# Attention scores of a two-block transformer: the low half of the keys read on 64 partitions instead of on 128 padded with zeros

## The reference

```python
# block 1: 8 query heads, 2 key heads, head dim 64, a window of 128 keys
scores = jnp.einsum("bnqhgd,bnkhd->bnhgqk", q, kw).astype(jnp.float32) * ATTN_SCALE
...
# block 2: 2 layers, 8 heads of head dim 64, chunks of 64, 8 chunks to the left
scores = jnp.einsum("bnqhd,bnkhd->bnhqk", qc, kb) * (dh ** -0.5)
...
scores = jnp.where(valid, scores + bias[None, None], NEG_INF)
p = jax.nn.softmax(scores, axis=-1)
```

## Time and profile before

| | |
|---|---|
| median of 3 runs | 1238.54 us (1238.12 to 1240.27) |
| the profiled execution, its own time | 1238.12 us |
| its span, first to last instruction | 1236.3 us |
| time outside the span | 1.8 us |
| PE busy | 1207.9 us, 98% of the span |
| DVE, ACT, POOL busy | 844.2, 555.0, 351.5 us |
| attention of block 1, layer 0 and layer 1 of block 2 | 54 to 108 us, 721 to 830 us, 992 to 1102 us |

### The profile page before, as it was taken

One profiled execution on the slowest core, in us unless ns is written; L12 is line 12 of the kernel. 1 busy time (PEld: TensorE's weight loads), 2 busy tenths in 40 slices (PEclk: granted clock), 3 DMA queues, 4 the chain that ended last, 5 costly groups with the idle time before them and its releaser, 6 DMA issues.

```text
span 1236.3 us, 15052 instructions
## 1 busy us (share of the span) xinstructions
PE 1207.9 (98%) x5844; PEld 1013.3 (82%) x5844; DVE 844.2 (68%) x1532; ACT 555.0 (45%) x965; POOL 351.5 (28%) x267
## 2 busy tenths in 40 slices
PE   7999999999989999999999899999999999999997
PEld 6888888888877888888888689888888889888886
DVE  6778433436788836663668967777967766778964
ACT  6667332324434313342434455644334556553433
POOL 0155000002299991000002763343103033342000
PEclk9999999999999999999999999999999999999999
DMA  5322233223323332333223242322122332222221
GB/s 193 106 69 69 85 103 99 89 85 104 109 69 98 107 102 85 102 102 97 80 75 107 86 129 87 92 89 92 61 85 86 120 102 86 87 86 93 72 74 69
DMA packets 36152, 115.33 MB, mean 93 GB/s; under 512 B 3824, under 2 KB 6384, under 8 KB 36080
## 3 DMA queue, kind: packets, MB, share of 16 engines
q1 hardware_dynamic: 36080, 114.36, 29.3%
HBM read 112.25 MB, written 2.10 MB: 92 GB/s over the span
## 4 chain that ended last, share of the span: by engine, by line
PE 67%; DVE 20%; ACT 8%; issue 3%; POOL 1%; DMA 1%; SPq 0%; ACTq 0%
PE ps L273 65%; DVE RA L250 8%; DVE FA L262 6%; DVE FA L250 5%; ACT RA L242 4%; ACT FA L247 1%; ACT RA L246 1%; POOL FA L250 1%; DVE FA L1269 1%; PE ps L1303 1%; ACT FA L246 1%; DMA FA<-x 1%; DVE RA L262 1%; PE ps L747 0%; DVE FA L1273 0%
## 5 line engine op out<-in xcount | busy, mean ns | idle before, releaser
L273 PE MATMUL ps<-RA 128*128 128x512 f32 (+3 forms) x5460 | 1179.0, 376 | 11.6 <-DVE RA L250 9.3
L273 PEld LDWEIGHTS ps<-RA 128*128 128x128 f32 x5460 | 970.6, 188 | 197.3 <-DVE RA L250 11.1
L250 DVE TENSOR_TENSOR RA<-FA,RA 128x1024 fp32r<-128x1024 f32 (+4 forms) x316 | 334.8, 1068 | 185.7 <-ACT RA L242 183.5
L242 ACT ACTIVATE RA<-FA 128x1024 fp32r<-128x1024 f32 (+6 forms) x336 | 279.1, 860 | 340.4 <-PE ps L273 159.1
L250 POOL TENSOR_TENSOR FA<-FA 128x512 f32<-128x512 f32 (+1 forms) x89 | 123.2, 1384 | 549.5 <-ACT FA L246 450.6
L266 POOL TENSOR_SCALAR FA<-FA 128x256 f32<-128x256 f32 (+2 forms) x117 | 146.9, 1266 | 189.4 <-DVE FA L270 188.3
L262 DVE SCALAR_TENSOR_TENSOR FA<-ps,FA 128x512 f32<-128x512 f32 (+3 forms) x137 | 98.0, 721 | 87.6 <-PE ps L273 44.9
L247 ACT ACTIVATE FA<-FA 128x512 f32<-128x512 f32 (+3 forms) x113 | 61.2, 543 | 98.7 <-DVE FA L1273 78.3
L262 DVE SCALAR_TENSOR_TENSOR FA<-FA 128x4 f32<-128x4 f32 (+4 forms) x166 | 87.5, 535 | 17.8 <-ACT FA L246 6.5
L246 ACT ACTIVATE FA<-ps,FA 128x512 f32<-128x512 f32 x61 | 41.6, 686 | 120.3 <-PE ps L273 120.2
L246 ACT ACTIVATE FA<-FA 128x512 f32<-128x512 f32 (+3 forms) x74 | 41.5, 568 | 63.0 <-DVE FA L262 56.1
(11 more groups left out here) (46 smaller groups left out, 306.4 us busy)
## 6 DMA issues: line engine op xcount, KB each, us to landing
FA<-w_units SPq DMA_DIRECT2D x190, 512.0 KB, 3.5
FA<-rel SPq DMA_DIRECT2D x16, 256.0 KB, 3.4
FA<-w_units SPq DMA_DIRECT2D x8, 384.0 KB, 3.0
FA<-x SPq DMA_DIRECT2D x4, 512.0 KB, 7.7
FA<-dmat SPq DMA_DIRECT2D x8, 256.0 KB, 3.2
out<-FA SPq DMA_DIRECT2D x8, 256.0 KB, 2.2
FA<-gain SPq DMA_DIRECT2D x1, 512.0 KB, 3.5
FA<-positions SPq DMA_DIRECT2D x1, 256.0 KB, 3.9
```

Of the source, the lines that this page charges most:

```text
L242: return lambda eng: eng.activation(dst, src, ACT.Copy)
L250: return lambda eng: eng.tensor_tensor(dst, a, b, op)
L273: return lambda e: e.matmul(dst, a, b, start=start, stop=stop_)
```

## The change

`stacked_scores` gets the number of the head and reads both operands of its second pass on 64 partitions only: the half that holds the queries' high part and the keys' low part. The other half no longer needs zeros, so head A's and head B's low keys lie in one K2 of 512 columns, on its two halves; the memsets, their helper and the waits for them go. The tiles move together by 1024 columns, and the program takes the default size for a scratch area of transfers issued by software, of which it has none, in place of 1024 bytes.

```diff
-QA, QB, K1A, K1B, VV = Z + 8192, Z + 10240, Z + 12288, Z + 12800, Z + 13824
-K2A, K2B = Z + 13312, Z + 25856
+QA, QB, K1A, K1B, K2, VV = Z + 8192, Z + 10240, Z + 12288, Z + 12800, Z + 13312, Z + 13824
...
-K2P = Z + 20480
-P2H, P2L = Z + 22528, Z + 24192
-YAH, YAL = Z + 25856, Z + 27904
-R_COLS = Z + 29952
+P2H, P2L = Z + 21504, Z + 23168
+YAH, YAL = Z + 24832, Z + 26880
+R_COLS = Z + 28928
...
-        def zero(name, c, n, after):
-            G(name, after, lambda e: e.memset(Rf(c, n), 0.0))
...
-        zero("z1a", K2A, 512, [])
-        zero("z1", K2B, 512, [])
...
-                V(f"{key}.l{n}", [f"{key}.h3", zeroed], fn)
+                V(f"{key}.l{n}", [f"{key}.h3"], fn)
...
-        def stacked_scores(o, q, k1, k2, i, k0, nk, after, name):
+        def stacked_scores(o, q, k1, k2, head, i, k0, nk, after, name):
+            p = 64 * head
             T(None, after, mmul(o, R(q + 128 * i, 128), R(k1 + k0, nk), True, False))
-            T(name, [], mmul(o, R(q + 128 * i, 128), R(k2 + k0, nk), False, True))
+            T(name, [], mmul(o, R(q + 128 * i, 128, p, p + 64), R(k2 + k0, nk, p, p + 64), False, True))
...
-        zero("z2", K2P, 2048, ["gemm.br7"])
...
-                base, lows = QK + 2048 * (i % 2), K2P + 1024 * (i % 2)
-                return [base + 512 * n for n in range(4)] + [lows, lows + 512]
+                base = QK + 2560 * (i % 2)
+                return [base + 512 * n for n in range(5)]
...
-    nc = _bacc.Bacc("TRN2", target_bir_lowering=False, num_devices=1, dynamic_dma_scratch_size=1024)
+    nc = _bacc.Bacc("TRN2", target_bir_lowering=False, num_devices=1)
```

More of the change, by code:

```diff
@@ L610, in stacked_q, with stacked_k @@
             free(f"bank{b}" if src is None else src[1], f"{key}.l1")
-        def stacked_k(key, b, k1a, k1b, k2a, k2b, after, zeroed, bias=None):
+        def stacked_k(key, b, k1a, k1b, k2, after, bias=None):
             n = 0
@@ L622, in stacked_k @@
             yield
-            for n, (k1, k2, p) in enumerate(((k1a, k2a, 0), (k1b, k2b, 64))):
+            for n, (k1, p) in enumerate(((k1a, 0), (k1b, 64))):
                 src = bank(b, 512, 0, p, p + 64)
@@ L687, in q_evacuate @@
             yield from stacked_q(f"q{m}", qb[m], QA + 512 * m, QB + 512 * m, [f"qn.{m}"], bin_ + m, src=(t, tn))
-        k_split = stacked_k("k", 5, K1A, K1B, K2A, K2B, ["gemm.k"], "z1", bin_ + 4)
+        k_split = stacked_k("k", 5, K1A, K1B, K2, ["gemm.k"], bin_ + 4)
         staggered([q_evacuate(0), q_evacuate(1), k_split, q_evacuate(2), q_evacuate(3)])
@@ L709, in a_scores @@
                     after = after + ["k.l1", "q3.l1"]
-                stacked_scores(bank(b, nk, 256 * (t % 2)), (QA, QB)[g] + 512 * t, (K1A, K1B)[g], (K2A, K2B)[g], n,
+                stacked_scores(bank(b, nk, 256 * (t % 2)), (QA, QB)[g] + 512 * t, (K1A, K1B)[g], K2, g, n,
                                k0, nk, after, f"S.{s}.{t}")
@@ L1197, in evac_qk @@
                     else:
-                        yield from stacked_k(key, b, cols[2], cols[3], cols[4], cols[5], after + room, "z2")
+                        yield from stacked_k(key, b, cols[2], cols[3], cols[4], after + room)
                     return
@@ L1243, in half_scores @@
                         after = after + [f"{l}q{item}.l1", f"{l}k{item}.l1"]
-                        stacked_scores(bank(b, w), cols[h % 2], cols[2 + h % 2], cols[4 + h % 2], i, 0, w, after, name)
+                        stacked_scores(bank(b, w), cols[h % 2], cols[2 + h % 2], cols[4], h % 2, i, 0, w, after, name)
                     else:
```

## The result

The changed kernel takes 1272.14 us (median of 4 runs, 1272.07 to 1272.27) against 1238.49 us: 33.65 us more, a ratio of 1.0271 with a 95% interval of 1.0256 to 1.0286. The forecast was 1258.0 us in a range of 1238.0 to 1289.5. The sign held and the time lies in the range, but the increase is 1.7 times the forecast one. The profile shown here is of another execution, of 1273.37 us.

A forecast was written before the change was run, and what follows sets the result against it. PE was taken to bound the kernel, almost without slack in the score stretches. The profiled 1238.12 us plus 20.7 for 192 changes of height, less 0.8 absorbed, gave 1258.0 us; memsets and addresses counted 0. Range: 1238.0 to 1289.5 us.

The forecast's parts named there:

- The price: Cost on PE of each of 192 changes between 128 and 64 rows in the score passes: 108 ns, together 20.7 us.
- the 0.8 us of absorption: PE's waits in the layers' score stretches, 0.4 us in each layer, would absorb 0.8 us of added time at most.
- The slot of block 1: Test stretch of block 1, from 98.31 to 106.51: its 8.20 us should become 9.06 us.
- the drain alone: At every change of height the old pass's 162 ns tail is paid: 31.1 us, 1268.4 us in all; chance 0.24.
- both: At every change of height the 162 ns tail and an exposed load, 270 ns: 51.8 us, 1289.1 us in all; chance 0.15.
- The middle value: At each change of height one weight load's distance is exposed, 108 ns: 20.7 us, 1258.0 us in all; chance 0.34.
- The row of transposes: Block 1's changes between transposes and fp32r passes cost 0 to 15 ns each; 192 times this is 0 to 2.9 us.
- One way only: Only one direction of the height change in score passes costs: 96 x 0.108 = 10.4 us, 1247.7 us in all; chance 0.07.
- nothing: Height of the second score passes only masks rows: 0 to 2.9 us more, 1238.1 to 1241.0 us; chance 0.16.
- faster: Second score passes of 64 rows take half of PE's time, 7.0 us less, if changes cost under 36 ns: 1231.1 us; chance 0.04.

The follow-up runs named there:

- e1_full_height: The changed kernel, but the second score pass reads all 128 partitions again: 1239.95 us, ratio 1.0004 to the kernel before.
- The grouped kernel: The changed kernel with score passes ordered as two of 128 rows, then two of 64, halving the changes of height to 96: 1254.77 us, ratio 1.0124.
- e5_positions: The grouped kernel, but the second of each group's two 64-row passes reads the other 64 partitions: 1248.99 us, ratio 1.0080 to the kernel before.

## Why the prediction was right, and where it was too small

*Where the time can come from.* Right: PE was the bound in the stretches with scores, memsets, addresses and waits were worth nothing (`e1_full_height`, 1.0004), and the cost is the number of changes of height times a price. The count of 192 stood, and half and 80 of them gave 15.7 and 12.5 us. One reading was looser than I told it: the 9s of the page's clock row mean 90% or more in each slice, and only the windows of the earlier trace rows say 1.00.

*The price.* This is the term that was mis-sized. I took 108 ns, an exposed weight load alone, and left out that the pass before must also give up part of its overlap. The range went from 0 to 270 ns a change, so that the time lies in it says little for the sum. Measured: 0.200 us behind and around passes of 256 columns (yardstick), and 33.65 / 192 = 0.175 us on the mean over all widths and after what is absorbed. 192 x 0.067 = 12.9 us is the difference to the forecast sum, of the 14.1 us by which 1272.14 lies above 1258.0; the rest is the 0.8 us of absorption, which the 0.175 already contains, and the 0.4 us between the profiled execution and the median.

The slot of block 1 that I had named as the test took 8.20 us. It now takes 107.43 - 97.67 = 9.76 us, where my forecast had 9.06, the drain alone 9.50 and both together 10.36:

```profile
97.67 1.03 PE L741 MATMUL ps<-FA 128*128 128x128 f32 x8
98.46 9.13 PE L271 MATMUL ps<-RA 128*128 128x256 f32 x36
107.43 1.04 PE L741 MATMUL ps<-FA 128*128 128x128 f32 x8
```

*Of what it consists.* The load is exposed, as I said: the passes behind a change last 98 to 106 ns longer than those of the earlier trace rows, and loads begin with their passes. But as much again comes on top, 0.200 - 0.098 = 0.10 us by which the next pass starts later than the longer one explains. The grouped kernel shows the two parts one after the other. Four passes of 256 columns at the start of its yardstick, the second of 128 rows, both of 64, and the next of 128, each from a timeline of its own:

```profile
77.77 0.28 PE L271 MATMUL ps<-RA 128*128 128x256 f32 x1
77.98 0.38 PE L271 MATMUL ps<-RA 64*128 64x256 f32 x1
78.20 0.28 PE L271 MATMUL ps<-RA 64*128 64x256 f32 x1
78.41 0.39 PE L271 MATMUL ps<-RA 128*128 128x256 f32 x1
```

The first pass of the other height comes 0.21 us behind its predecessor, 0.09 more than 0.120, and the pass behind it, of the same height, 0.22 us, 0.10 more. The second part is the exposed load, which shows as the longer first pass (0.38 instead of 0.28). The first part I read as the old pass leaving the array before the new load may go in; the rows show that the load waits, not what it waits for. I had this as the rival "both", with 162 ns for that part, the whole overlap of two passes, and gave it 0.15. Its mechanism fits, its tail was too large by 60 to 70 ns. The middle value came as near as it did because it had one of the two parts at its right size. The rule of the Trainium skill that I set against my sum, in "TensorEngine Tiling (Array Packing)", section "Key Properties", that a change of mode but not of tile drains the engine, agrees with the runs in both halves: 64 rows between 128 cost 0.200 us a change, the other 64 rows (`e5_positions`) cost nothing.

*Why I took the small price.* The row of transposes, two changes of kind for 0.03 us, spoke for a low price, and I said it was near only in name. That holds: transposes and fp32r passes both use 128 rows, so the row says nothing of a change of height. It was no reason for a low price.

*By width.* Where a pass has only 128 columns its neighbour's load was, as I read it, already partly exposed before, so a change adds less: the duration rises from 255 ns to 324, 69 ns, against 98 to 106 with wider ones. Hence block 1, mostly 256 columns, has 11.6 / 64 = 0.181 us a change.

*One way only; nothing; faster.* "One way only" falls by durations that are equal in both directions, "nothing" by the result. "Faster" had something true in it: the half-used array does let two passes run at once (`e5_positions`), but they were two of the small height at different positions, and a change costs more than the 36 ns up to which it would have paid.

*Absorption.* In each layer PE's waits of 0.4 us vanished as forecast. Where layer 0's retention follows I had looked for none. There 129.5 us before are 129.2 us after, 0.3 us less, windows of the kernel before and of the changed one:

```profile
829.80:959.30 129.50, 127.54 (x617) 106.70 (x616) 100.27 (x187) 54.27 (x94) 27.37 (x20) 1.00 0.26 80
```

```profile
854.00:983.20 129.20, 127.67 (x616) 106.76 (x616) 99.38 (x185) 52.61 (x90) 24.61 (x18) 1.00 0.26 80
```

One instruction of difference between the windows makes that 0.1 to 0.3 us, too little to matter.

## What to carry to other kernels

Padding a contraction of 64 with zeros up to the 128 partitions of its neighbours was the faster way here. The zeros cost 2.8 us of an idle POOL once; the short passes cost up to 0.2 us of PE at each change to them and back. If short passes must be mixed in, keep them together and count the changes, not the passes. Count only the changes across the border that matters: 96 rows beside 128 were free, 64 and 32 were about equally dear.

## What the runs showed of the hardware

Two 64-row passes on different halves of the array, writing to different banks, start and load together: 96 loads of 183 ns in 8.9 us. I had given this no place in the prediction. The Trainium skill has it in "TensorE: Matmul & The Clock Gate", section "Part 3: Packing small matmuls — row/col tiling", where tiles on different rows overlap with a few ns between their starts; the trace of `e5_positions` agrees.

PE's clock can fall to 1.2 GHz in the midst of a busy stretch, in one execution and not in the next. The same 3.3 us of work in `e1_full_height` and in the kernel before, 9 passes against 17:

```profile
683.50:686.80 3.30, 3.30 (x9) 2.57 (x8) 3.09 (x10) 0.00 (x0) 0.68 (x4) 0.50 0.39 102
```

```profile
683.60:686.90 3.30, 3.30 (x17) 2.81 (x18) 3.20 (x8) 0.44 (x1) 1.61 (x3) 1.00 0.18 22
```

It costs up to 8 x 0.227 = 1.8 us each time where PE is the bound. The changed kernel's profile has two such stretches as well, which the page's row of 40 slices, all 9, does not show:

```profile
375.30:378.70 3.40, 3.40 (x9) 2.67 (x8) 3.33 (x6) 0.69 (x2) 3.24 (x3) 0.50 0.61 177
696.10:699.50 3.40, 3.40 (x11) 2.72 (x9) 3.23 (x10) 0.13 (x1) 0.57 (x3) 0.50 0.25 67
```

What PE waited for before doesn't tell the two profiles apart. From 675 to 684 us, in `e1_full_height` and then in the kernel before:

```profile
PE ps L455 <- POOL FA L248: 1.9, 1, 1.9
```

```profile
PE ps L457 <- POOL FA L250: 1.9, 1, 1.9
```

Both idled for 1.9 us, and the clock fell in one. What decides is open. It isn't the kernel alone: of 21 executions of the kernel before on one chip, eleven had a mean granted clock of 0.996 or 0.997 and took 1239.07 to 1240.32 us, ten had 0.998 to 1.0 and took 1237.41 to 1238.89 us. An effect of over 0.1% that comes and goes is why differences of a few tenths of a per cent need several runs.
